# Turning the modulation rows with transposes and adding their four strips on VectorE

## The chip, the cores and the metric

The kernel runs on one core of a Trainium2 chip. The metric is the device time of one execution in microseconds; the number compared is the median of several runs.

## The reference

One layer of a hybrid backbone: a parallel mix of long convolution, latent attention and pooling, over 512 latent tokens and 256 context tokens, width 2048. The part that matters here is the modulation ahead of the first projection. For the conditioning vector `c` and for a learned one, `c_ctx`, three vectors come out of one weight matrix, and the normed tokens are scaled and shifted by them before `w_in`:

```python
def adaln(cond, w_ada, b_ada):
    mod = jax.nn.silu(cond) @ w_ada + b_ada
    shift, scale, gate = jnp.split(mod[:, None, :], 3, axis=-1)
    return shift, scale, gate
...
sh, sc, gt = adaln(c, w_ada[l], b_ada[l])
sh_c, sc_c, gt_c = adaln(c_ctx[None], w_ada[l], b_ada[l])
h_l = rmsnorm(x_l, norm_g[l]) * (1.0 + sc) + sh
h_c = rmsnorm(x_c, norm_g[l]) * (1.0 + sc_c) + sh_c
u_l = h_l @ w_in[l]
u_c = h_c @ w_in[l][:, OFF_KV:OFF_MLA_G]
```

## The kernel before

**Tiling.** Width 2048 is cut into 16 blocks (KT) of 128. The tokens lie transposed, a block j being 128 partitions by 512 tokens (`x_tile(j)`, in UG) and 256 context tokens (`c_tile(j)`). Every value that goes through TensorE in exact products is split into a high part and a low part of reduced type: ScalarE writes the high one, VectorE (or GpSimd) the low one by subtraction. Three products of such parts make one tile product.

**The stage concerned** is the first 130 us. A step j = 0 to 15 makes five tile products on TensorE (`tile(i, j)`, lines 1891 and 1897) for the columns of w_in that keys and queries need. The step takes `a_hi` and `a_lo` (tokens times scale, high and low), `hc_hi` and `hc_lo` (context), and `wa_hi` and `wa_lo` (weights). Norm and shifts are put in afterwards, so VectorE also keeps sums of squares (`rstd`, `rstd_c`) and sums of weights times shift (`shifted`, line 1211). From step 11 on ScalarE and VectorE also make the tokens for the next stage: `scale` (line 1240), `h_hi` on ScalarE (line 664), `h_lo` on VectorE (line 1247), two blocks a step.

**Modulation.** For a block b the weights (1 or 2 MB) come by DMA into one of three buffers `ada`. `ada_vectors(b)` on TensorE (line 1872) makes 16 products. Each has 32 columns of silu(c) as its stationary side, of which two are used (c and c_ctx), and goes to one of four strips of 32 partitions of bank ps[7]. So row 32s + r of the bank holds the part of strip s for vector r, and the four strips have to be added and the rows turned into a column per block. ScalarE copies the rows to SBUF (`rows_out`, `mod_rows`, line 670). Then `combine(b)` on TensorE (lines 1880 and 1881) does both at once: rows, stationary, times `comb`, a 128x2 matrix that selects and adds. ScalarE turns the result into scale and shift (`modulation`, lines 682 and 673), and then makes a_hi (line 637) and hc_hi. Blocks 0 and 1 (EARLY = 2) bring the scale alone, and their shifts come in one more block, number 12 (LATE), by `late_shifts`. Therefore `block_of(j)` is j up to 11 and j + 1 from 12 on.

**Order.** Every engine works through its own list in the order of the code, and waits on semaphores. On TensorE tile(0, j) is followed by `ada_vectors` of the next step's block and tile(1, j), then `combine` of it, then tiles 2 to 4. In step 10 the LATE block is done too. `at_work(n)` issues n idle products on ones, whose result nobody reads. At the start TensorE does four of them, `hidden(0)` (line 1917, the first layer of the filter network, which waits for `first_in` and for `feats`, shown as filter_steps), and ada_vectors(0), with two idle products in the middle.

On VectorE a step is: a_lo, hc_lo, the shifts, the sums, then h_lo of two blocks and `scale` of two. At the start it works on the sine arguments of the filter network (`hidden`, `reduced`, lines 1268 to 1277) ahead of the first a_lo. On GpSimd stands only wa_lo (line 577) in this stage. SP issues nearly all DMAs; ScalarE's queue issues the filter steps and the identity (lines 628 and 629). All loads of a step wait for the buffers of an earlier one.

The two lines of the combination before:

```python
if b >= EARLY:
    eng.matmul(ps[7][:, 0:2], rows[:, 0:P], comb[:], start=True, stop=True)
eng.matmul(ps[7][:, 2:4], rows[:, P:2 * P], comb[:], start=True, stop=True).then_inc(comb_mm, 1)
```

## Time and profile before

| | |
|---|---|
| median of 3 runs | 931.52 us (930.85 to 931.66) |
| profiled execution | 934.35 us, of which span 932.5 us |
| TensorE products busy | 916.4 us (98% of the span) |
| VectorE, ScalarE, GpSimd busy | 640.6, 395.8, 99.6 us |
| the 16 DMA engines, first 100 us | busy throughout, 367 to 423 GB/s |

The profile is of one execution; its times count from the start of the span. Each product of the float32 type shows as two instructions in the trace, a transpose as one. The ends of products are modelled, so the start of one to the start of the next says more than a duration.

### The profile page before, as it was taken

The page shows a single profiled execution, that of the slowest core. Times are in us where ns is not written, and L with a number is a line of the kernel's source. Part 1 is how long each engine was busy: PE and PEld are TensorE (multiplying, and loading weights), DVE is VectorE, ACT ScalarE, POOL GpSimd, SP SyncE. Part 2 cuts the span into 40 slices and gives each one's busy share as a digit, 9 for nine tenths or more (in the row PEclk, how much of TensorE's full clock was granted, in tenths as well). Part 3 has the DMA queues.
Part 4 walks back from the last instruction along what each step waited for, and adds up shares of the span by engine and source line. Part 5 has one row for each costly group of instructions (what it writes and reads, how often), then busy time and mean ns, then how long its engine had stood idle before and what let it go on. Part 6 is the DMA issues. An engine that isn't in the chain of part 4 may idle for free.

```text
span 932.5 us, 12223 instructions
## 1 busy us (share of the span) xinstructions
PE 916.4 (98%) x4878; PEld 760.6 (82%) x4878; DVE 640.6 (69%) x834; ACT 395.8 (42%) x614; POOL 99.6 (11%) x78
## 2 busy tenths in 40 slices
PE   9999999999999999999999999999999999999996
PEld 6777788888888888887788888889899888888885
DVE  5575997799987899855965854877777961424244
ACT  4654656535435443332234333554544541322124
POOL 2222200300003000000005720000000000202020
PEclk9999999999999999999999999999999999999998
DMA  9999923222322222476772251101010244233214
GB/s 367 414 419 423 401 104 102 91 79 95 110 79 91 69 85 74 148 292 225 269 287 90 91 175 52 57 23 57 1 57 1 91 171 191 91 102 119 96 46 181
DMA packets 29685, 137.88 MB, mean 148 GB/s; under 512 B 3483, under 2 KB 3995, under 8 KB 22716
## 3 DMA queue, kind: packets, MB, share of 16 engines
q1 hardware_dynamic: 29152, 136.44, 39.3%
q8 instruction: 39, 0.64, 0.3%
q10 hardware_dynamic: 476, 0.66, 0.2%
q14 instruction: 18, 0.15, 0.1%
HBM read 131.84 MB, written 4.19 MB: 146 GB/s over the span
## 4 chain that ended last, share of the span: by engine, by line
PE 87%; DVE 5%; DMA 3%; ACT 2%; issue 2%; POOLq 0%; SPq 0%; ACTq 0%
PE pp L1975 34%; PE pp L2289 19%; PE pp L2005 16%; PE pp L1891 6%; PE pp L1872 3%; DMA w_raw<-in_wb_dram 2%; PE pp L2252 2%; PE pp L1897 2%; DVE gate_acc L1329 1%; PE pp L2244 1%; PE pp L2243 1%; ACT U L962 1%; ACT w_hi L754 1%; DVE softmax_stats L1597 1%; DVE pt_lo L1612 0%
## 5 line engine op out<-in xcount | busy, mean ns | idle before, releaser
L1975 PE MATMUL pp<-h_hi,w_hi 128*128 128x512 f32 x544 | 213.9, 393 | 2.5 <-DVE w_lo L1317 2.4
L1975 PE MATMUL pp<-h_hi,w_lo 128*128 128x512 f32 x544 | 211.9, 389 | 0.0
L1975 PE MATMUL pp<-h_lo,w_hi 128*128 128x512 f32 x544 | 211.8, 389 | 0.0
L1317 DVE TENSOR_TENSOR w_lo<-w_raw,w_hi 128x1024 fp32r<-128x1024 f32 x68 | 88.0, 1295 | 77.9 <-ACT w_hi L754 77.4
L754 ACT ACTIVATE w_hi<-w_raw 128x1024 fp32r<-128x1024 f32 x68 | 71.8, 1056 | 141.6 <-PE pp L1975 90.1
L1975 PEld LDWEIGHTS pp<-h_hi,w_hi 128*128 128x128 f32 x544 | 102.2, 188 | 25.3 <-DVE w_lo L1317 4.4
L1975 PEld LDWEIGHTS pp<-h_hi,w_lo 128*128 128x128 f32 x544 | 102.1, 188 | 21.7
L1975 PEld LDWEIGHTS pp<-h_lo,w_hi 128*128 128x128 f32 x544 | 102.2, 188 | 20.5 <-issue 0.2
L2289 PE MATMUL pp<-wo_hi,m_hi 128*128 128x512 f32 x256 | 100.5, 393 | 0.0
L1632 DVE TENSOR_TENSOR wo_lo<-wo_raw,wo_hi 128x2048 fp32r<-128x2048 f32 x16 | 36.7, 2291 | 92.7 <-ACT wo_hi L993 92.7
L2289 PE MATMUL pp<-wo_hi,m_lo 128*128 128x512 f32 x256 | 99.6, 389 | 0.0
L2289 PE MATMUL pp<-wo_lo,m_hi 128*128 128x512 f32 x256 | 99.6, 389 | 0.0
L993 ACT ACTIVATE wo_hi<-wo_raw 128x2048 fp32r<-128x2048 f32 x16 | 30.6, 1915 | 89.4 <-PE pp L2289 89.4
L2289 PEld LDWEIGHTS pp<-wo_lo,m_hi 128*128 128x128 f32 x256 | 48.1, 188 | 10.3 <-issue 0.5
L2289 PEld LDWEIGHTS pp<-wo_hi,m_hi 128*128 128x128 f32 x256 | 48.1, 188 | 10.3 <-issue 0.5
L2289 PEld LDWEIGHTS pp<-wo_hi,m_lo 128*128 128x128 f32 x256 | 48.0, 188 | 10.1
L619 POOL TENSOR_TENSOR y<-y,gain 128x512 f32<-128x512 f32 x12 | 15.5, 1297 | 335.5 <-ACT out_tmp L1000 335.2
L1612 DVE TENSOR_TENSOR pt_lo<-pp,pt_hi 128x768 fp32r<-128x768 f32 x32 | 30.5, 953 | 24.9 <-ACT pt_hi L970 24.8
L970 ACT ACTIVATE pt_hi<-pp 128x768 fp32r<-128x768 f32 x32 | 26.0, 812 | 49.1 <-PE pp L2252 49.1
L962 ACT ACTIVATE U<-pp,softmax_stats 128x768 f32<-128x768 f32 x32 | 28.9, 903 | 27.5 <-DVE softmax_stats L1599 27.4
L1891 PE MATMUL pp<-a_hi,wa_hi 128*128 128x512 f32 x80 | 35.4, 443 | 0.0
L1329 DVE SCALAR_TENSOR_TENSOR gate_acc<-w_gate_raw,silu_c,gate_acc 128x2048 f32<-128x2048 f32 x15 | 35.2, 2346 | 0.0
(330 smaller groups left out, 1792.6 us busy)
## 6 DMA issues: line engine op xcount, KB each, us to landing
w_raw<-in_wb_dram SPq DMA_DIRECT2D x68, 512.0 KB, 3.3
ada_raw<-in_w_ada_dram SPq DMA_DIRECT2D x15, 2048.0 KB, 12.9
w_gate_raw<-in_w_gate_dram SPq DMA_DIRECT2D x16, 1024.0 KB, 5.1
wo_raw<-in_w_out_dram SPq DMA_DIRECT2D x16, 1024.0 KB, 4.7
wa_raw<-in_wa_dram SPq DMA_DIRECT2D x14, 320.0 KB, 7.3
y<-in_x_dram SPq DMA_DIRECT2D x4, 1024.0 KB, 7.9
UG<-in_xT_dram SPq DMA_DIRECT2D x7, 512.0 KB, 7.9
wh_raw<-in_w_heads_dram SPq DMA_DIRECT2D x4, 768.0 KB, 4.4
```

Of the source, the lines that this page charges most:

```text
L754: eng.activation(lane(wb_hi, n % 2), lane(wb_raw, n % KW), ACT.Copy).then_inc(wb_hi_done, 1)
L962: eng.activation(prob(n % 3).rearrange("p (a b) -> p a b", a=2), psum[:, 2 * (n % 2):2 * (n % 2) + 2, 0:384], ACT.Exp, bias=st[:, 4 * s + ...
L993: eng.activation(wo_high_[n % 2][:], wo_raw[n % 3][:], ACT.Copy).then_inc(wo_hi, 1)
L1317: eng.tensor_tensor(lane(wb_lo, n % KW), lane(wb_raw, n % KW), lane(wb_hi, n % 2), ALU.subtract).then_inc(wb_lo_done, 1)
L1329: eng.scalar_tensor_tensor(out=gate_acc[:], in0=w, scalar=c, in1=gate_acc[:], op0=ALU.mult, op1=ALU.add).then_inc(row_sums, 1)
L1612: eng.tensor_tensor(lo, psum[:, 4:6, :].rearrange("p a b -> p (a b)")[:, 0:LK].rearrange("p (k q) -> p k q", k=6), hi, ALU.subtract).then_ ...
L1632: eng.tensor_tensor(wo_low_[n % 3][:], wo_raw[n % 3][:], wo_high_[n % 2][:], ALU.subtract).then_inc(wo_lo, 1)
L1872: mm = eng.matmul(ps[7][32 * strip:32 * strip + 32, 256 - n:256], spread[:, 32 * kk:32 * kk + 32], ada[b % 3][:, kk * n:(kk + 1) * n], sta ...
L1891: mm = eng.matmul(ps[i][:], w, x, start=first and n == 0, stop=last and n == 2)
L1975: mm = eng.matmul(ps[i][:], w, x, start=(kk == 0 and m == 0), stop=(kk == KT - 1 and m == 2))
L2005: mm = eng.matmul(dst, w, x, start=first and m == 0, stop=last and m == 2)
L2289: mm = eng.matmul(psum[:, 4 * (b % 2) + tok, :], a, v[:, w:w + L], start=(kk == 0 and m == 0), stop=(kk == 15 and m == 2))
```

## The change

`combine(b)` now transposes the rows as they are, against the identity, into 128 or 256 columns of the same bank. A new function `strips(b)` on VectorE adds the four strips with one reduction into a small SBUF tile `strip_sums`, which ScalarE reads instead of PSUM. ScalarE's modulation waits for that sum. TensorE waits for the identity ahead of the first modulation products instead of in step 1; of its idle products one goes away in the middle of ada_vectors(0), and two are added behind it. The first half of the first scale weights is issued at the head of ScalarE's queue, no longer second on SP's.

```diff
@@ -98,7 +98,7 @@
         first_in, silu_c = alloc("first_in", 2 * KT + 131 + N_PAR + 2), alloc("silu_c", 2 * KT)
         cond, hf = first_in[:, 0:2 * KT], first_in[:, 2 * KT:2 * KT + 131]
         par, comb = first_in[:, 2 * KT + 131:2 * KT + 131 + N_PAR], first_in[:, 2 * KT + 131 + N_PAR:]
-        mod, scale_bias = alloc("mod", 4 * KT), alloc("scale_bias", KT)
+        mod, scale_bias, strip_sums = alloc("mod", 4 * KT), alloc("scale_bias", KT), alloc("strip_sums", 4)
         nrm, small, shift_cols = alloc("nrm", 8), alloc("hy_small", 8), alloc("shift_cols", 8)
         psum = ctx.enter_context(nc.psum_tensor("pp", [P, 8, 512], F32))
         ps = [psum[:, i, :] for i in range(8)]
@@ -312,7 +312,7 @@
 
         a_hi_done, a_lo_done = sem("a_hi_done"), sem("a_lo_done")
         root_done = sem("root_done")
-        ada_mm, rows_done, comb_mm = sem("ada_mm"), sem("rows_done"), sem("comb_mm")
+        ada_mm, rows_done, comb_mm, strips_done = sem("ada_mm"), sem("rows_done"), sem("comb_mm"), sem("strips_summed")
         mod_done, mod_scale, first_x_in, scaled = sem("mod_done"), sem("mod_scale"), sem("first_x_in"), sem("scaled")
         h_hi_done, h_lo_done = sem("h_hi_done"), sem("h_lo_done")
         wa_hi_done, wa_lo_done = sem("wa_hi_done"), sem("wa_lo_done")
@@ -416,7 +416,6 @@
                     eng.wait_ge(row_sums, shifts_of(j - 2))
                 eng.dma_start(wa_raw(j), t["wa"][j, :, :]).then_inc(wa_in[j % 2], 16)
 
-            eng.dma_start(ada[0][:, 0:1024], t["w_scale"][0, :, 0:1024]).then_inc(ada_in[0], 16)
             eng.dma_start(ada[0][:, 1024:2048], t["w_scale"][0, :, 1024:2048]).then_inc(hf_in, 16)
             load_wa(0)
             eng.dma_start(UG[:, 0:L], t["xT"][:, 0:L]).then_inc(first_x_in, 16)
@@ -625,6 +624,7 @@
 
         @block.scalar
         def _(eng):
+            eng.dma_start(ada[0][:, 0:1024], t["w_scale"][0, :, 0:1024]).then_inc(ada_in[0], 16)
             eng.dma_start(feats, t["feats"]).then_inc(feat_in, 16)
             eng.dma_start(mem["ident"][:], t["ident"]).then_inc(ident_in, 16)
 
@@ -670,22 +670,22 @@
                 eng.activation(rows[:, a:256], ps[7][:, a:256], ACT.Copy).then_inc(rows_done, 1)
 
             def shift_of(k, at_column):
-                eng.activation(mod[:, 4 * k:4 * k + 2], ps[7][:, at_column:at_column + 2], ACT.Identity,
+                eng.activation(mod[:, 4 * k:4 * k + 2], strip_sums[:, at_column:at_column + 2], ACT.Identity,
                                bias=par[:, P_BSH + k:P_BSH + k + 1], scale=1.0).then_inc(mod_done, 1)
 
             def modulation(j):
 
-                eng.wait_ge(comb_mm, block_of(j) + 1)
+                eng.wait_ge(strips_done, block_of(j) + 1)
                 if j in (10, 11):
 
                     eng.wait_ge(sum_mm, j - 9)
-                eng.activation(mod[:, 4 * j + 2:4 * j + 4], ps[7][:, 2:4], ACT.Identity, bias=scale_bias[:, j:j + 1],
+                eng.activation(mod[:, 4 * j + 2:4 * j + 4], strip_sums[:, 2:4], ACT.Identity, bias=scale_bias[:, j:j + 1],
                                scale=par[:, P_NG + j:P_NG + j + 1]).then_inc(mod_scale, 1)
                 if j >= EARLY:
                     shift_of(j, 0)
 
             def late_shifts():
-                eng.wait_ge(comb_mm, LATE + 1)
+                eng.wait_ge(strips_done, LATE + 1)
                 for k in range(EARLY):
                     shift_of(k, 2 * k)
 
@@ -1276,12 +1276,28 @@
                     link(eng.scalar_tensor_tensor(out=a, in0=r, scalar=-part, in1=a, op0=ALU.mult, op1=ALU.add))
                 eng.tensor_scalar(a, a, -PI_MAX, PI_MAX, ALU.max, ALU.min).then_inc(mlp_arg, 1)
 
+            def strips(b):
+                eng.wait_ge(comb_mm, b + 1)
+                if b:
+                    eng.wait_ge(mod_scale, b - (b > LATE))
+                if b > EARLY:
+                    eng.wait_ge(mod_done, b - EARLY + (EARLY - 1) * (b > LATE))
+                if b in (10, 11):
+                    eng.wait_ge(sum_mm, b - 9)
+                h = 1 if b < EARLY else 0
+                x = ps[7][:, h * P:2 * P].rearrange("p (h s r) -> p h r s", h=2 - h, s=4)[:, :, 0:2, :]
+                eng.tensor_reduce(strip_sums[:, 2 * h:4].rearrange("p (h r) -> p h r", r=2), x, AX.X, ALU.add).then_inc(strips_done, 1)
+
             hidden(0)
             reduced(0)
+            strips(0)
             first_tokens(0)
             first_context(0)
+            strips(1)
             hidden(1)
             for j in range(KT - 1):
+                if j:
+                    strips(block_of(j + 1))
                 first_tokens(j + 1)
                 first_context(j + 1)
                 if j == 0:
@@ -1309,6 +1325,7 @@
                     scale(2 * j - 20)
                     scale(2 * j - 19)
                 if j + 2 == LATE:
+                    strips(LATE)
                     for k in range(EARLY):
                         shifted(k)
 
@@ -1866,7 +1883,7 @@
                 n = P if b < EARLY else 256
                 for kk in range(KT):
                     if b == 0 and kk == 8:
-                        at_work(2)
+                        at_work(1)
                         eng.wait_ge(hf_in, 16)
                     strip = kk % 4
                     mm = eng.matmul(ps[7][32 * strip:32 * strip + 32, 256 - n:256], spread[:, 32 * kk:32 * kk + 32],
@@ -1877,8 +1894,8 @@
             def combine(b):
                 eng.wait_ge(rows_done, b + 1)
                 if b >= EARLY:
-                    eng.matmul(ps[7][:, 0:2], rows[:, 0:P], comb[:], start=True, stop=True)
-                eng.matmul(ps[7][:, 2:4], rows[:, P:2 * P], comb[:], start=True, stop=True).then_inc(comb_mm, 1)
+                    eng.transpose(ps[7][:, 0:P], rows[:, 0:P], mem["ident"][:])
+                eng.transpose(ps[7][:, P:2 * P], rows[:, P:2 * P], mem["ident"][:]).then_inc(comb_mm, 1)
 
             def tile(i, j):
                 first, last, s = j == 0, j == KT - 1, j % 2
@@ -1923,7 +1940,9 @@
             at_work(4)
             hidden(0)
             eng.wait_ge(silu_done, 2)
+            eng.wait_ge(ident_in, 16)
             ada_vectors(0)
+            at_work(2)
             combine(0)
             at_work(4)
             for j in range(KT):
@@ -1933,8 +1952,6 @@
                 else:
                     eng.wait_ge(wa_hi_done, 1)
                     eng.wait_ge(a_hi_done, 1)
-                if j == 1:
-                    eng.wait_ge(ident_in, 16)
                 for i in range(A_TILES):
                     if i == 2 and j:
                         eng.wait_ge(a_lo_done, 2 * j + 2)
```

On TensorE at the start, before; ada_raw_64 are the first scale weights, ones the idle products:

```order
L1872 MATMUL pp<-ada_raw_64,silu_spread 32x128 x8
L1857 MATMUL pp<-ones 128x128 x2
L1872 MATMUL pp<-ada_raw_64,silu_spread 32x128 x8
L1881 MATMUL pp<-first_in,mod_rows 128x2
L1857 MATMUL pp<-ones 128x128 x4
```

And the same place after:

```order
L1889 MATMUL pp<-ada_raw_64,silu_spread 32x128 x8
L1874 MATMUL pp<-ones 128x128
L1889 MATMUL pp<-ada_raw_64,silu_spread 32x128 x8
L1874 MATMUL pp<-ones 128x128 x2
L1898 MATMUL pp<-ident,mod_rows 128x128
L1874 MATMUL pp<-ones 128x128 x4
```

One idle product has moved behind the modulation products and one is added there, so two stand ahead of the combination, which has become a transpose.

On VectorE between steps 10 and 12, before; h_tmp<-UG is `scale`, the shifts on wa_first are the late ones:

```order
L1240 SCALAR_TENSOR_TENSOR h_tmp<-UG,mod,rstd 128x512 x2
L1211 SCALAR_TENSOR_TENSOR shift_x<-wa_first,mod,shift_x 128x640
L1211 SCALAR_TENSOR_TENSOR shift_c<-wa_first,mod,shift_c 128x384
L1211 SCALAR_TENSOR_TENSOR shift_x<-wa_first,mod,shift_x 128x640
L1211 SCALAR_TENSOR_TENSOR shift_c<-wa_first,mod,shift_c 128x384
L1191 SCALAR_TENSOR_TENSOR a_lo<-UG,mod,a_hi 128x512
```

And the same place after:

```order
L1240 SCALAR_TENSOR_TENSOR h_tmp<-UG,mod,rstd 128x512 x2
L1289 TENSOR_REDUCE strip_sums<-pp 128x4
L1211 SCALAR_TENSOR_TENSOR shift_x<-wa_first,mod,shift_x 128x640
L1211 SCALAR_TENSOR_TENSOR shift_c<-wa_first,mod,shift_c 128x384
L1211 SCALAR_TENSOR_TENSOR shift_x<-wa_first,mod,shift_x 128x640
L1211 SCALAR_TENSOR_TENSOR shift_c<-wa_first,mod,shift_c 128x384
L1289 TENSOR_REDUCE strip_sums<-pp 128x4
L1191 SCALAR_TENSOR_TENSOR a_lo<-UG,mod,a_hi 128x512
```

Two reductions stand there now: that of the LATE block between the scales and the late shifts, and that of block 13 directly ahead of step 12's a_lo.

On VectorE from step 12's h_lo to step 13's a_lo, after (before, the same rows without the reduction; steps 14 and 15 are alike):

```order
L1247 SCALAR_TENSOR_TENSOR h_lo<-h_tmp,mod,h_hi 128x512 x2
L1240 SCALAR_TENSOR_TENSOR h_tmp<-UG,mod,rstd 128x512 x2
L1289 TENSOR_REDUCE strip_sums<-pp 128x4
L1191 SCALAR_TENSOR_TENSOR a_lo<-UG,mod,a_hi 128x512
L1198 SCALAR_TENSOR_TENSOR hc_lo<-c_raw,mod,hc_hi 128x256
```

The reduction stands behind all of the work of the step before.

## Rows read from the trace of the kernel before

**Rows 1.** Two stretches: length; busy us (instructions) by engine; clock; DMA share; GB/s.
```profile
4.00:5.00 1.00, 1.00 (x2) 0.00 (x0) 0.00 (x0) 0.01 (x1) 0.00 (x0) 1.00 0.95 322
96.00:112.00 16.00, 16.00 (x146) 11.57 (x138) 15.87 (x21) 9.08 (x20) 5.29 (x3) 1.00 0.99 407
```

**Rows 2.** The chain that ended last: start us, us, what.
```profile
1.17 4.33 DMA ada_raw<-in_w_scale_dram
...
15.93 1.00 PE pp L1920 x2
...
58.94 0.12 PE pp L1880 x2
59.06 0.22 PE pp L1881 x2
59.28 0.80 PE pp L1891 x3
...
80.08 0.12 PE pp L1880 x2
...
101.50 0.69 PE pp L1891 x3
...
122.64 1.39 PE pp L1891 x6
```

**Rows 3.** VectorE in order of time: start us, us, instruction, idle time before.
```profile
95.66 0.88 DVE L1211 SCALAR_TENSOR_TENSOR shift_x<-wa_first,mod,shift_x 128x640 f32<-128x640 f32 x1
...
99.84 0.75 DVE L1191 SCALAR_TENSOR_TENSOR a_lo<-UG,mod,a_hi 128x512 fp32r<-128x512 f32 x1
...
102.56 2.70 DVE L1247 SCALAR_TENSOR_TENSOR h_lo<-h_tmp,mod,h_hi 128x512 fp32r<-128x512 f32 x2
...
106.56 0.75 DVE L1191 SCALAR_TENSOR_TENSOR a_lo<-UG,mod,a_hi 128x512 fp32r<-128x512 f32 x1
...
113.60 0.75 DVE L1191 SCALAR_TENSOR_TENSOR a_lo<-UG,mod,a_hi 128x512 fp32r<-128x512 f32 x1 [0.29 <-ACT a_hi L637]
...
120.81 0.74 DVE L1191 SCALAR_TENSOR_TENSOR a_lo<-UG,mod,a_hi 128x512 fp32r<-128x512 f32 x1
...
123.20 1.40 DVE L1247 SCALAR_TENSOR_TENSOR h_lo<-h_tmp,mod,h_hi 128x512 fp32r<-128x512 f32 x2
```

**Rows 4.** The chain of the attention stage: six transposes of 128x128.
```profile
608.92 0.65 PE pp L2252 x6
```

**Rows 5.** ScalarE in order of time around 79 us.
```profile
78.36 0.74 ACT L696 ACTIVATE wa_hi<-wa_raw 128x640 fp32r<-128x640 f32 x1 [2.00 <-DMA wa_raw<-in_wa_dram]
79.25 0.39 ACT L670 ACTIVATE mod_rows<-pp 128x256 f32<-128x256 f32 x1 [0.16 <-PE pp L1872]
```

**Rows 6.** All engines in order of time at the start.
```profile
0.73 0.62 ACTq L628 DMA_DIRECT2D filter_steps<-in_feats_dram  x1
...
3.45 1.96 PE L1917 MATMUL pp<-filter_steps,first_in 33*64 33x512 f32 x2 [0.33 <-DMA first_in<-in_first_dram]
5.45 0.80 DVE L1268 TENSOR_SCALAR filter_steps<-pp,first_in 64x512 f32<-64x512 f32 x1 [1.85 <-PE pp L1917]
...
6.64 1.22 PE L1857 MATMUL pp<-ones 128*128 128x128 f32 x4
...
9.35 0.42 DVE L1277 TENSOR_SCALAR filter_steps<-filter_steps 64x512 f32<-64x512 f32 x1
...
9.96 0.35 ACT L682 ACTIVATE mod<-pp,scale_bias,first_in 128x2 f32<-128x2 f32 x1
```

**Rows 7.** ScalarE in order of time: a modulation in the late steps.
```profile
112.38 0.35 ACT L682 ACTIVATE mod<-pp,scale_bias,first_in 128x2 f32<-128x2 f32 x1 [0.82 <-PE pp L1881]
```

**Rows 8.** Two groups on softmax_stats: duration ns min/median/max, first and last start, forms.
```profile
L1597 DVE TENSOR_REDUCE softmax_stats<-pp x32: 945/952/959, 577.2 to 742.9; 128x1 f32<-128x768 f32 x32
L1599 DVE TENSOR_SCALAR softmax_stats<-softmax_stats x32: 153/154/156, 578.2 to 743.9; 128x1 f32<-128x1 f32 x32
```

**Rows 9.** GpSimd in order of time beside VectorE's h_lo.
```profile
102.42 1.63 POOL L577 TENSOR_TENSOR wa_lo<-wa_raw,wa_hi 128x640 fp32r<-128x640 f32 x1 [4.45 <-ACT wa_hi L696]
```

## The prediction

> **What bounds the kernel now.** I read three views: busy time by stretch, the chain that ended last, and each engine's instructions in order of time. The change touches only the first 130 us, the stage in which sixteen steps j build the modulation vectors and the first projections; what follows is fed by TensorE without a gap, so a delay at the end of the stage goes into the total undiminished.
>
> Two engines are full in the last part of it. From 96 to 112 us TensorE is busy for 16.00 of 16 us and VectorE for 15.87 [rows 1]. The chain of waits goes through TensorE: the tile products of step 12 start at 101.50 and those of step 15 at 122.64, so one step takes 7.05 [rows 2]. VectorE is nearly as tight: it starts a_lo of steps 12, 13, 14 and 15 at 99.84, 106.56, 113.60 and 120.81, and only the third of them names an idle time, 0.29 [rows 3]. TensorE needs that a_lo (ready 0.7 after its start) at 101.50, 108.55 and so on: the slack is 1.0 to 1.3 us. So two questions decide: what TensorE saves, and what VectorE's order now costs.
>
> **Combination on TensorE.** Before, two float32 products with two columns each take 0.12 + 0.22 us, and the tile products behind them take 0.80 where three others take 0.69: 0.45 in all [rows 2]. After, two transposes stand there. The kernel has the same form elsewhere, six in 0.65 us, 0.11 each [rows 4]. That is 0.22, and up to 0.33 if the products behind them are late as before. The gain is 0.12 to 0.23 per combination; I take 0.18, 2.7 us for the 15 combinations with both halves.
>
> **How much of this arrives by 88 us.** The weights wa_raw come by DMA. In the step near 78 us ScalarE waited 2.00 us for them and began at 78.36, and the row copy behind it began at 79.25, 0.16 after ScalarE fell free [rows 5]. TensorE needs that copy for its next combination at 80.08 [rows 2], and the copy takes 0.39: 0.44 us later than now it would be late. If TensorE runs ahead of the DMA, which is busy throughout, it can be at most 0.16 + 0.44, about 0.55 us, ahead there; then it waits for the row copy. Two more combinations up to 88 us bring 0.36, so I take 0.9 as the lead at the combination of block 11. Bounds: 1.5 if the DMA also comes earlier, or a delay of 0.5 if the start loses much (next part).
>
> **The start.** The first half of the scale weights moves from SP's queue to the head of ScalarE's, ahead of the filter steps and the identity. It needed 4.33 us from its issue at 1.17 to landing [rows 2]. It may now be issued at 0.73, where ScalarE's queue starts [rows 6], worth up to 0.44. But hidden(0) waits for the filter steps, which now lie behind 512 KB. It ran from 3.45 [rows 6]; with the pace of 322 GB/s at 4 to 5 us [rows 1], 512 KB more ahead of the steps take 1.6, so they come at about 5.0. Bounds: 3.45 if they overtake, 5.7 if SP's queue takes turns. The Trainium skill (DMA: Bandwidth & Descriptors, Queues, rings and completion order) says that each DMA engine goes round-robin between the queue rows that have work, packet by packet. By that rule the transfer would share the engines with SP's second half and take nearly twice as long, and the filter steps would come at the late bound. No row here shows such sharing of large transfers.
>
> From there two paths run. hidden(0) takes 1.96, and VectorE's sine arguments on 64 rows run from 5.45 to 9.77 [rows 6]; the new strips(0) stands behind them, so the modulation begins at about 5.0 + 1.97 + 4.35 + 0.25 = 11.6, against 9.96. On TensorE ada_vectors(0) follows hidden(0) and the new wait for the identity: start 1.5 later, one idle product less in its middle (-0.6, half of the 1.22 of two [rows 6]), two more before the combination (+0.6, as they take 1.2 and the row copy hid 0.4 of it anyway), one product fewer. That meets the other path at about 11.2. So the first tile products start about 1.6 later than now. Of this some comes back, since TensorE runs at half pace at first: hidden(0) takes 1.96 at 3.45, and hidden(1), of as many columns, 1.00 at 15.93 [rows 2, 6]. TensorE has fewer gaps after the filter steps now, and I count 0.7 back. At j = 1 VectorE comes to strips(2) only after its sums, 0.3 more. Net +1.2 at 27 us. Nine combinations then bring 1.6, and TensorE is 0.4 to 0.55 ahead at 79 us: the cap of the part before is just reached, so this loss is mostly hidden by waiting that the DMA would have forced anyway.
>
> The Trainium skill (TensorE: Matmul & The Clock Gate, Part 4) adds that transposes do not count as activity for the clock. By that rule the start would stay slow longer; see the rivals.
>
> **VectorE's new place in the chain.** strips(b) is queued behind everything that VectorE does for the step before. In steps up to 11 that costs little: VectorE is idle when the combination comes, and the 0.2 to 0.25 falls into a slack of 1 us. From step 10's end on it isn't idle. Before, ScalarE made mod and a_hi while VectorE still worked, and a_lo followed at once. Now VectorE finishes the two scale() instructions, then sums the strips, then must wait for ScalarE's modulation and a_hi before a_lo. Behind it are queued the shifts, sums and h_lo of the step, so nothing fills the gap.
>
> The price of one such gap: the modulation began at 112.38 and a_lo at 113.60, 1.22 [rows 3, 7]. The sum of strips: no row shows a reduction of 16 elements. Lower bound 0.15 (128x1, SBUF), upper 0.95 (768 elements from PSUM) [rows 8]; I take 0.20, near the small one, and 0.05 for the hand-over. ScalarE now reads SBUF instead of PSUM, which I credit with 0.05. Gap: 1.4 (1.2 to 1.6 with half of the doubt on either side).
>
> Now the steps, relative to the lead of 0.9. VectorE's path in step 11 gains 0.25 before the scales. strips(LATE) and the first late shift that waits for it put shifted(0), now at 95.66 [rows 3], 0.5 later: ScalarE's late shifts, the first of them about as long as a modulation (0.35 [rows 7]), now stand behind VectorE's scales, and TensorE's ada_vectors(13) waits for them too, but no longer than VectorE's path below. So shifted(0) is 0.75 late. Then a_lo of step 12: 99.84 + 0.75 + 1.4 = 102.0, late by 2.15. Step 13: 6.72 of work between starts, plus 1.4, 110.1 (late by 3.55). Step 14: 6.75 of work (7.04 less the 0.29), 118.3 (4.7). Step 15: 7.21 of work, 126.9 (6.1). The work does not shrink: the pair of h_lo instructions takes 2.70 while GpSimd's wa_lo runs beside it from 102.42, and 1.40 at 123.20 without it [rows 3, 9]; GpSimd still starts after ScalarE's h_hi, so the two still meet.
>
> TensorE can start step 15 at 126.9 + 0.70 = 127.6 instead of 122.64, +4.95. Less the lead of 0.9: +4.05. What TensorE would save in steps 11 to 15 vanishes, since it waits for VectorE. VectorE is 1.1 nearer to TensorE after that, and I add 0.1 for the change to the next stage. **Sum: +4.2 us.** The profiled execution was 934.35 (span 932.5 and 1.85 around it), so it would be 938.5; the median of the runs lay 2.8 lower at 931.52, so the forecast is 935.7. A measurement of this kernel can tell about 0.2% (1.9 us) from no change: 929.7 to 933.4 counts as the same.
>
> **Rivals.** First, the start costs more: the filter steps at 5.7 and nothing back from the pace give +2.6 and a delay instead of a lead at 88 us, about 1.4 to 2.4 worse: 937.5. For it: everything at the start hangs on one small transfer. Against: the DMA cap hides a part.
>
> Second, on the other side: the gap on VectorE is covered. If a_lo needs no more than its slack of 1.0 to 1.3 in steps 12 to 15, for instance because GpSimd's subtraction now falls into VectorE's waiting and gives 1.3 back per step, the gap of 1.4 is paid by that and only TensorE's savings remain: 0.9, about 0.3 more in each of steps 12 to 15 less the waits, some 1 us faster: 930.5. It decides at a gap of 0.35, the spare of 7.05 against 6.72. For it: contention of 1.3 is there. Against: the order of ScalarE and GpSimd moves with VectorE's.
>
> Third, the cover is partial (half of the steps): +1.5, 933.0.
>
> Fourth, TensorE stays at its lower pace up to the combination of step 3, since transposes keep it up less than products do: half pace from 15 to 21 us costs 6, of which the cap hides little: 939.5 and more.
>
> Fifth, the transposes save nothing (0.45 again). It changes the lead to 0, and so the time to 936.6; it lies inside my range.
>
> **Chances.** Forecast (with the fifth) 0.72; first 0.10; second 0.07; third 0.07; fourth 0.04. The forecast's own range is a gap of 1.2 to 1.6 over five places (1.0 each way) and a lead of 1.5 to -0.5: 934.1 to 938.1. With the first case and the upper part of the third it is 933.0 to 938.3, which leaves out the second, the fourth and half of the third. Slower by over 0.2%: 0.84; the same: 0.09; faster: 0.07.
>
> **What would show it.** Right: in the profile after, VectorE idles before each a_lo of steps 12 to 15, about 1.2 us released by ScalarE's a_hi, directly behind the reduction, and TensorE waits for a_lo in steps 12 to 15, some 1.3 us apiece; transposes at 0.11 spacing; a wait for the filter steps at the start. Wrong: TensorE's steps stay 7.05 or less apart up to 123 us, or h_lo pairs shrink to 1.40.

## The result, and the profile of the changed kernel

The changed kernel takes 940.69 us (median of four: 937.12, 942.23, 942.03, 939.35), the kernel before 931.59 beside it. The ratio on record, formed from all executions and not from the two medians, is 1.009 (95% interval 1.0071 to 1.011): slower, with the predicted sign, but by 9.1 us where 4.2 were forecast, and outside the range of 933.0 to 938.3. Five executions of the later runs that lasted over 1,000 us (two of the kernel before, two of e12, one of e10) are left out of every number here.

The profiled execution took 937.12, the shortest of the four; that of before took 934.35, which is 2.8 above its median. So the two profiles differ by only 2.8 us while the medians differ by 9.1. Two questions follow: what happens in the first 140 us, and what makes a profile and a median differ. I begin with the stage.

The longest waits of TensorE in the profile after (line waiting, what it waited for, us in total, times, longest):

```profile
PE pp L1908 <- DVE a_lo L1191: 4.3, 4, 1.6
PE pp L1934 <- DMA filter_steps<-in_feats_dram: 3.1, 1, 3.1
...
PE pp L1889 <- ACT mod L673: 1.6, 1, 1.6
```

The first row is for the most part the predicted one. Of its four waits for VectorE's a_lo, three are those of steps 13, 14 and 15 (1.08, 1.07 and 1.62); the fourth, 0.52, is that of step 2. In step 12 TensorE does not wait for a_lo, where the prediction had a wait of some 1.3: its loss lies a little earlier, in the third row, the wait for the late shifts in step 11 (1.59), which the prediction named and gave no time of its own.

VectorE's instructions of step 12 and the beginning of 13, in order of time (start, us, line, operation; in brackets the idle time before, and what ended it). Beside the rows of before [rows 3]:

```profile
105.06 2.70 DVE L1247 SCALAR_TENSOR_TENSOR h_lo<-h_tmp,mod,h_hi 128x512 fp32r<-128x512 f32 x2
107.68 1.40 DVE L1240 SCALAR_TENSOR_TENSOR h_tmp<-UG,mod,rstd 128x512 f32<-128x512 f32 x2
109.00 0.16 DVE L1289 TENSOR_REDUCE strip_sums<-pp 128x4 f32<-128x16 f32 x1
110.46 0.75 DVE L1191 SCALAR_TENSOR_TENSOR a_lo<-UG,mod,a_hi 128x512 fp32r<-128x512 f32 x1 [1.29 <-ACT a_hi L637]
```

The reduction takes 0.16, and then VectorE stands idle for 1.29. From the start of the reduction to the start of a_lo it is 1.46, where before a_lo followed the scales with no gap. The same idle time, 1.29, stands before a_lo in each of the steps 12 to 15. The chain of waits walks through exactly this gap (start, us, what):

```profile
109.08 0.09 DVE strip_sums L1289
...
109.20 0.39 ACT mod L682
109.59 0.07 ACT mod L673
...
109.70 0.73 ACT a_hi L637
...
110.46 0.46 DVE a_lo L1191
```

VectorE hands a sum of 16 numbers per partition to ScalarE, ScalarE makes scale, shift and a_hi, and VectorE, which could have worked on something else, waits at a_lo. The four a_lo of steps 12 to 15 start at 102.33, 110.46, 118.59 and 127.26 (before 99.84, 106.56, 113.60, 120.81), so the step has grown from 7.0 to 8.1 and once 8.7. Step 15 and the end of the stage, from the chain of waits after:

```profile
128.16 1.62 PE pp L1908 x6
129.79 1.95 PE pp L1927 x16
...
135.43 4.79 PE pp L1992 x21
```

Step 15 begins at 128.16 instead of 122.64 [rows 2], 5.5 later, and the next stage at 135.43 instead of 129.39, 6.0 later.

The combination has become cheaper, as TensorE's rows for block 7 show:

```profile
57.33 1.93 PE L1889 MATMUL pp<-ada_raw,silu_spread 128*32 128x256 f32 x32
...
59.99 0.27 PE L1897 MATMUL pp<-ident,mod_rows 128*128 128x128 f32 x1
60.10 0.27 PE L1898 MATMUL pp<-ident,mod_rows 128*128 128x128 f32 x1
60.13 0.48 PE L1908 MATMUL pp<-a_hi,wa_hi 128*128 128x512 f32 x1
...
64.14 1.93 PE L1889 MATMUL pp<-ada_raw,silu_spread 128*32 128x256 f32 x32
71.14 1.93 PE L1889 MATMUL pp<-ada_raw,silu_spread 128*32 128x256 f32 x32
78.16 1.93 PE L1889 MATMUL pp<-ada_raw,silu_spread 128*32 128x256 f32 x32
```

The transposes start 0.11 apart, and the modulation products of two neighbouring steps 6.82 apart (57.33 to 64.14) where it was 7.05: 0.22 a step. But the next two steps are 7.00 and 7.02 again, and the granted clock is at its upper level (2.4 GHz) in all of this stretch. Something else sets the pace from 64 us to 78 us; the experiments e6 and e10 find it.

The start, as TensorE and ScalarE lived it (rows of before: [rows 6]):

```profile
4.76 0.23 ACT L699 ACTIVATE silu_c<-first_in 128x32 f32<-128x32 f32 x1 [1.25 <-DMA first_in<-in_first_dram]
6.17 1.94 PE L1934 MATMUL pp<-filter_steps,first_in 33*64 33x512 f32 x2 [3.05 <-DMA filter_steps<-in_feats_dram]
8.42 1.08 PE L1889 MATMUL pp<-ada_raw,silu_spread 128*32 128x128 f32 x16 [0.32 <-issue]
...
13.97 0.47 PE L1908 MATMUL pp<-a_hi,wa_hi 128*128 128x512 f32 x1 [0.77 <-ACT a_hi L637]
...
15.09 1.08 PE L1889 MATMUL pp<-ada_raw,silu_spread 128*32 128x128 f32 x32
...
28.85 0.47 PE L1908 MATMUL pp<-a_hi,wa_hi 128*128 128x512 f32 x1 [0.52 <-DVE a_lo L1191]
```

hidden(0) waits 3.05 for the filter steps and starts at 6.17 instead of 3.45. The first tile products come at 13.97, before at 11.43: 2.5 later. The modulation products of block 1 take 1.08 at 15.09. Before, the same products at 12.99 took 1.94, half that pace, so 0.9 comes back here, and 0.4 with the three tile products ahead of them (1.12 from 13.97 to 15.09, before 1.56 from 11.43 to 12.99). The start of block 2's products is then 1.25 late (22.14 against 20.89). Then two steps lose time again: at 28.85 TensorE waits for the a_lo of step 2, since VectorE's sum of block 2's strips (at 26.49, a_lo at 27.95) stood behind the long work on sines and squares. At the products of block 3 the changed kernel is 1.8 late (29.72 against 27.94).

### The profile page after: what moved, and what is told of

Same layout as the page of the kernel before. It is cut to its first block, busy times and chain, and to the rows that moved or that the text cites. A ratio compares the mean times of both kernels' runs of the same rounds, so it can differ in the third digit from the quotient of the medians.

```text
span 935.3 us, 12197 instructions
## 1 busy us (share of the span) xinstructions
PE 912.0 (98%) x4848; PEld 755.7 (81%) x4848; DVE 642.1 (69%) x851; ACT 396.0 (42%) x614; POOL 101.8 (11%) x78
## 4 chain that ended last, share of the span: by engine, by line
PE 80%; DVE 6%; ACT 2%; issue 2%; POOLq 0%; DVEq 0%; ACTq 0%
PE pp L1992 38%; PE pp L2306 19%; PE pp L2022 16%; PE pp L2269 2%; DVE h_lo L1247 1%; PE pp L2261 1%; PE pp L2260 1%; ACT U L962 1%; DVE softmax_stats L1614 1%; DVE pt_lo L1629 0%; PE pp L2091 0%; PE pp L1908 0%; PE pp L2039 0%; PE pp L2038 0%; PE pp L2144 0%
## 6 DMA issues: line engine op xcount, KB each, us to landing
ada_raw<-in_w_ada_dram SPq DMA_DIRECT2D x15, 2048.0 KB, 12.6
```

## Experiments

All times are medians, with the number of executions, and the ratio against executions of the kernel before on the same chip (formed from all executions, so it is not quite the quotient of the medians). "Stage" is how much later than before (140.38) ScalarE starts one fixed instruction behind the stage, the w_hi of line 754 that stands directly ahead of the single w_hi of line 824 (w_hi is the high part of the next projection's weights). It is read from one profile of each. How far one profile can be trusted is seen in e5 and e12, whose code is that of before up to step 15: their last modulation products start at 116.42 and 116.37 where those of before start at 116.22. So 0.2 in this column is nothing, and the three profiles of the changed kernel differ by 2.2. The two kernels that appear again (e1 and e11, e12) are repeats.

| kernel | median, executions | ratio (95%) | stage |
|---|---|---|---|
| changed | 940.69 (4) | 1.009 (1.0071 to 1.011) | +6.05 |
| e1, changed again | 939.05 (6) | 1.0082 (1.0054 to 1.011) | +6.39 |
| e11, changed, third | 940.04 (6) | 1.0086 (1.0055 to 1.0117) | +8.25 |
| e3, combination alone | 939.05 (6) | 1.0069 (1.0041 to 1.0096) | +5.57 |
| e4, sum before the scales | 933.17 (12) | 1.0017 (0.9999 to 1.0035) | +0.72 |
| e2, start alone | 932.92 (12) | 1.0015 (0.9999 to 1.0032) | +1.21 |
| e7, first load alone | 933.18 (10) | 1.0013 (1.0004 to 1.0022) | +2.31 |
| e6, combination, sum early | 931.3 (11) | 1.0 (0.9984 to 1.0016) | +0.08 |
| e8, e4 and load behind the filter steps | 934.39 (11) | 1.0031 (1.0015 to 1.0046) | +2.16 |
| e5, delay only | 937.09 (5) | 1.0058 (1.0046 to 1.007) | +6.02 |
| e12, delay again | 938.28 (8) | 1.006 (1.004 to 1.0079) | +5.96 |
| e9, before with half loads | 930.61 (10) | 0.9985 (0.9967 to 1.0003) | -0.27 |
| e10, e6 with half loads | 931.17 (9) | 0.9982 (0.9963 to 1.0001) | -0.52 |

### e1: the changed kernel again

No edit. It is the same code in the company of the next three.

> The changed kernel once more, unaltered. Its first four runs spread over 5 us (937.1 to 942.2), while those of the kernel before spread over 1. Theory D (VectorE's order alone is the cause): a constant cost of 5.5 us at the last step's tile products, so runs near 937 to 939 and a spread of about 1. Theory S (a part of the cost is made anew in every run at the start, by the pace of TensorE or of the first transfers): the spread of some 5 us comes back, the median near 940.5, and in a profile of a slow run the first step or two start later than 13.97 and 22.14 us.

Measured: 938.39, 938.55, 945.02, 939.55, 938.0, 939.65. The stage loses 6.39, a_lo of steps 12 to 15 at 102.67, 110.82, 118.95 and 127.61. The stage's loss repeats in this profile, which is of the execution of 938.39. Where the spread of seven microseconds comes from it doesn't show. A spread of about 1 (Theory D) is refuted, but the median is not at 940.5 either (Theory S); e11 takes that up.

### e2 and e3: the start alone, the combination alone

e2 has the start of the changed kernel and the combination of before:

```diff
-            eng.dma_start(ada[0][:, 0:1024], t["w_scale"][0, :, 0:1024]).then_inc(ada_in[0], 16)
...
         def _(eng):
+            eng.dma_start(ada[0][:, 0:1024], t["w_scale"][0, :, 0:1024]).then_inc(ada_in[0], 16)
             eng.dma_start(feats, t["feats"]).then_inc(feat_in, 16)
...
-                        at_work(2)
+                        at_work(1)
...
+            eng.wait_ge(ident_in, 16)
             ada_vectors(0)
+            at_work(2)
```

> The kernel before with the start of the changed one alone: first scale weights at the head of ScalarE's queue, wait for the identity ahead of ada_vectors(0), one idle product in its middle and two behind it; the combination is still the product with comb. Theory D: the start costs at most 1 us in the median and adds no spread, 931.5 to 932.5. Theory S: +2.5 us or more (the first tile products start near 14.0 instead of 11.43), and the spread of some 4 us is here, so 934 to 936.

e3 is the changed kernel with these lines put back (the load leaves ScalarE's queue again), the wait for the identity directly ahead of combine(0):

```diff
+            eng.dma_start(ada[0][:, 0:1024], t["w_scale"][0, :, 0:1024]).then_inc(ada_in[0], 16)
...
-                        at_work(1)
+                        at_work(2)
...
-            eng.wait_ge(ident_in, 16)
             ada_vectors(0)
-            at_work(2)
+            eng.wait_ge(ident_in, 16)
             combine(0)
```

> The transposes and VectorE's sum alone: first scale weights on SP's queue and two idle products in the middle as before, none ahead of the combination; the wait for the identity stands directly ahead of the first combination, which needs it now. Theory D: nearly all of the loss stays, VectorE idles 1.29 us before a_lo in steps 12 to 15, about +4.2 us, 935.7. Theory S: +3 us at most (the gaps less the savings on TensorE), with a spread below 1.5.

e2 takes 932.92 (1.0015), its stage loses 1.21. This lies between the two theories: 1.4 in the median, more than 1 and less than 2.5, and its executions spread from 932.08 to 937.18. Its steps in the last part are 7.05 as before (a_lo at 100.96, 107.75, 114.80, 122.02), hidden(0) waits 2.9 for the filter steps, and block 1's products have the full pace early:

```profile
14.98 1.08 PE L1872 MATMUL pp<-ada_raw,silu_spread 128*32 128x128 f32 x32
```

e3 takes 939.05 (1.0069), its stage loses 5.57, more than either theory had (4.2 and at most 3). TensorE's waits in it:

```profile
PE pp L1908 <- DVE a_lo L1191: 4.2, 4, 1.6
PE pp L1889 <- DMA ada_raw<-in_w_ada_dram: 1.1, 1, 1.1
```

So nearly the whole loss belongs to the combination. The second row is new: without the loss at the start, TensorE comes to block 9's weights 1.1 before they have landed. The first profile of the whole change names no such wait, since there TensorE comes late from the start. The two parts don't add up (5.57 + 1.21 = 6.8 against 6.05 to 6.4), because the loss at the start is partly waiting that the DMA forces anyway: the changed kernel is 1.95 behind e3 at the products of block 3 (29.72 against 27.77) and 0.77 behind at those of block 9 (71.14 against 70.37).

### e4: the sums ahead of the scales

This keeps everything of the change but VectorE's order from the end of step 10 on. The sum of the next step's strips moves from behind the two `scale` instructions to ahead of them, that of the LATE block too, and that of block 13 to between the two late shifts:

```diff
-                if j:
+                if 0 < j < 11:
                     strips(block_of(j + 1))
...
+                if j + 2 == LATE:
+                    strips(LATE)
+                if 10 < j < KT - 2:
+                    strips(block_of(j + 2))
                 if j >= 10:
                     scale(2 * j - 20)
                     scale(2 * j - 19)
                 if j + 2 == LATE:
-                    strips(LATE)
-                    for k in range(EARLY):
-                        shifted(k)
+                    shifted(0)
+                    strips(block_of(j + 2))
+                    shifted(1)
```

> The changed kernel, but from block 12 on VectorE sums the strips ahead of the two scales (and for block 13 between the two late shifts) instead of behind them, so that ScalarE makes scale and a_hi while VectorE still works; nothing else is moved. Theory D: the idle time before a_lo of steps 12 to 15 falls from 1.29 to under 0.4 and the time by about 5 us. Theory S: the same idle time goes, but some 3 us and the spread remain, so near 935.5.

It takes 933.17 (1.0017), and the stage loses 0.72 instead of 6.05. VectorE's rows at the place that was shown above:

```profile
106.30 0.16 DVE L1289 TENSOR_REDUCE strip_sums<-pp 128x4 f32<-128x16 f32 x1
106.38 1.40 DVE L1240 SCALAR_TENSOR_TENSOR h_tmp<-UG,mod,rstd 128x512 f32<-128x512 f32 x2
107.76 0.75 DVE L1191 SCALAR_TENSOR_TENSOR a_lo<-UG,mod,a_hi 128x512 fp32r<-128x512 f32 x1
```

```profile
PE pp L1912 <- DVE a_lo L1191: 0.5, 1, 0.5
```

The same reduction, with the same 0.16, but now 1.40 of scales lie between it and a_lo, ScalarE's 1.2 us run beside them, and a_lo has no idle time before it. Of TensorE's four waits for a_lo only that of step 2 is left, 0.5, so those of steps 13 to 15 (3.8 together) are gone, and the wait for the late shifts has shrunk from 1.59 to 0.34. These two make 5.0 of the 5.3 us of stage that the order is worth. The instructions are the same, only in another order. As the order was changed in all these places at once, what each is worth alone is not shown.

### e5: is a delay at the end of the stage passed on undiminished?

The kernel before with 26 idle products ahead of step 15's tiles:

```diff
+                if j == KT - 1:
+                    for _ in range(26):
+                        eng.matmul(ps[7][:, 0:P], ones[:], ones[:], start=True, stop=True)
```

> The kernel before with 26 idle products on TensorE ahead of step 15's first tile products, which nobody reads: a bare delay of some 5.5 us at the place where the changed kernel had collected it, with nothing else changed. Theory P (a delay at the end of the stage is passed on undiminished, and the stage with the gate weights at 404 to 490 us adds its own, random part that has nothing to do with the change): the fastest run is 5.5 above the fastest of before (930.8), 936.3, and the median lies 1 to 2 above that. Theory M (the later stages absorb or multiply a delay): the fastest run is under 935 or over 938.

It takes 937.09 (1.0058; 936.88 to 937.62), 5.3 more than before on the same chip (931.82) with a delay of 6.0 in the stage. The median lies only 0.2 above the shortest, not 1 to 2 as Theory P had it. The shortest ones differ by 6.0 (936.88 and 930.85). So a delay of this size is passed on nearly one to one, and a pure delay of the changed kernel's size gives 937, not 940.7. At this point it seemed that the change cost 2 to 3 us beyond its delay. e12 weakens that.

### e6, e8: what the transposes are worth

e6 is the kernel before with transposes, strip sums in e4's order, and the start as it was, but for the wait for the identity, which stands ahead of the first combination. Its main edit against before:

```diff
-                    eng.matmul(ps[7][:, 0:2], rows[:, 0:P], comb[:], start=True, stop=True)
-                eng.matmul(ps[7][:, 2:4], rows[:, P:2 * P], comb[:], start=True, stop=True).then_inc(comb_mm, 1)
+                    eng.transpose(ps[7][:, 0:P], rows[:, 0:P], mem["ident"][:])
+                eng.transpose(ps[7][:, P:2 * P], rows[:, P:2 * P], mem["ident"][:]).then_inc(comb_mm, 1)
```

> The transposes with VectorE's sum ahead of the scales, and the start as in the kernel before. If the start is the last loss of the version with the early sum (+0.7 at the end of the stage with the changed start), this one should end the stage 0.3 to 1.0 us ahead of the kernel before: 930.0 to 931.3. If the DMA of the modulation weights caps the lead (they land as late as before), it is at the kernel before within 0.4.

It takes 931.3 (1.0, 0.9984 to 1.0016): no gain, though steps of 6.82 in place of 7.05 save 0.22 each. TensorE at block 9's weights:

```profile
70.84 1.93 PE L1893 MATMUL pp<-ada_raw,silu_spread 128*32 128x256 f32 x32 [1.35 <-DMA ada_raw<-in_w_ada_dram]
```

Without the wait these products would have started at 69.5, 0.7 ahead of before (70.21). Their weights were issued 0.26 earlier than before (56.63 against 56.89), but took 14.1 instead of 12.9:

```profile
ada_raw<-in_w_ada_dram SPq DMA_DIRECT2D x1, 2048.0 KB, 14.1
```

They landed at 70.73, and a lead of 0.7 became a delay of 0.6. The later steps win that back, and the stage ends 0.08 later than before. The saving is real, and the wait for the DMA takes it back.

e8 is e4 (the changed start with its wait for the identity ahead of ada_vectors(0)) with the filter steps put at the head of ScalarE's queue, then the scale weights, then the identity:

```diff
+            eng.dma_start(feats, t["feats"]).then_inc(feat_in, 16)
             eng.dma_start(ada[0][:, 0:1024], t["w_scale"][0, :, 0:1024]).then_inc(ada_in[0], 16)
-            eng.dma_start(feats, t["feats"]).then_inc(feat_in, 16)
             eng.dma_start(mem["ident"][:], t["ident"]).then_inc(ident_in, 16)
```

> The changed kernel with the early sum, and on ScalarE's queue the filter steps first, then the scale weights, then the identity. Theory Q: hidden(0) starts at 3.6 to 4.2, the modulation products wait for the identity, which now is last (about 6), and the first steps are some 1.5 us earlier than in the version with the filter steps second. Time: 930.0 to 931.5, unless the DMA caps the lead.

934.39 (1.0031), where 930.0 to 931.5 had been expected. The identity was expected at about 6 and came at 8.4, so the wait has only changed its name:

```profile
3.37 1.96 PE L1938 MATMUL pp<-filter_steps,first_in 33*64 33x512 f32 x2 [0.26 <-DMA first_in<-in_first_dram]
...
8.43 1.08 PE L1893 MATMUL pp<-ada_raw,silu_spread 128*32 128x128 f32 x16 [3.10 <-DMA ident<-in_ident_dram]
```

hidden(0) is back at 3.37, and the identity, now the small load behind the large one, keeps ada_vectors(0) until 8.43, the same time as in the changed kernel (8.42). In the changed kernel the identity lands at 8.34 too, just behind the end of hidden(0), so two small loads are late there and bringing one forward gains nothing.

### e7: the load alone, without the idle products

```diff
-            eng.dma_start(ada[0][:, 0:1024], t["w_scale"][0, :, 0:1024]).then_inc(ada_in[0], 16)
...
         def _(eng):
+            eng.dma_start(ada[0][:, 0:1024], t["w_scale"][0, :, 0:1024]).then_inc(ada_in[0], 16)
             eng.dma_start(feats, t["feats"]).then_inc(feat_in, 16)
```

> The kernel before with one edit: the first half of the first scale weights at the head of ScalarE's queue, ahead of the filter steps and the identity. Theory Q (the two queues take turns, and the filter steps lie behind 512 KB): hidden(0) starts at about 6.1 instead of 3.45 and the stage ends about 1.2 late, 932.7: the whole of the start's cost. If instead the idle products and the identity make it, under 0.4 late.

```profile
4.98 0.23 ACT L699 ACTIVATE silu_c<-first_in 128x32 f32<-128x32 f32 x1 [1.48 <-DMA first_in<-in_first_dram]
5.90 1.94 PE L1917 MATMUL pp<-filter_steps,first_in 33*64 33x512 f32 x2 [2.79 <-DMA filter_steps<-in_feats_dram]
...
15.12 1.94 PE L1872 MATMUL pp<-ada_raw,silu_spread 128*32 128x128 f32 x32
```

933.18 (1.0013), stage +2.31 in the profile, where 1.2 had been expected. The queue move alone delays the filter steps as in the changed kernel, and it is most of the cost of the start: ada_vectors(0) begins at 7.77, 2.1 later than before (5.63), in the changed kernel 2.8 later. There hidden(0) itself is 0.3 later than in e7, and 0.3 more lies between its end and ada_vectors(0), which waits for the identity that lands at 8.34. The other half of that part, the identity's wait and the idle products, seems the good one: with it (e2) block 1's products take 1.08, without it 1.94 (at 15.12). But this pace changes from one execution to the next. In e5 and e12, whose start is that of the kernel before (1.94), the same products take 1.08 and 1.36:

```profile
13.59 1.08 PE L1872 MATMUL pp<-ada_raw,silu_spread 128*32 128x128 f32 x32 [0.26 <-DMA ada_raw<-in_w_scale_dram]
```

```profile
13.24 1.36 PE L1872 MATMUL pp<-ada_raw,silu_spread 128*32 128x128 f32 x32
```

All six profiles with the changed idle products and wait have 1.08; of the eight without them one has. So this half makes the full pace the rule there. Of the 0.9 that came back in the changed kernel, the comparison with e5 would leave nothing. In the profiles of e2 and e7 the difference is 1.1 us of stage; in the medians of twelve and ten executions it isn't seen (932.92 against 933.18).

### e9 and e10: is it the modulation weights that hold the pace?

Both load only half of each block's 2 MB, and the products of the second half read the first half again, so blocks from 2 on come out with other values; all instructions stay. e9 is the kernel before with this, e10 is e6 with it.

```diff
-                dst, src = (ada[b % 3][:, 0:2048], t["w_scale"][b]) if b < EARLY else (ada[b % 3][:], t["w_ada"][b - EARLY])
+                dst, src = (ada[b % 3][:, 0:2048], t["w_scale"][b]) if b < EARLY else (ada[b % 3][:, 0:2048], t["w_ada"][b - EARLY][:, 0:2048])
...
-                                    ada[b % 3][:, kk * n:(kk + 1) * n], start=kk < 4, stop=kk >= KT - 4,
+                                    ada[b % 3][:, kk * n % 2048:kk * n % 2048 + n], start=kk < 4, stop=kk >= KT - 4,
```

> The kernel before, but of each 2 MB block of modulation weights only the first half is loaded, and the products of its second half use the first again (the modulation is wrong in value, all instructions stay). Theory C (the modulation weights' arrival is the only thing that keeps TensorE from running ahead between 60 and 80 us, and in the kernel before it is just hidden): steps stay 7.05 apart and the stage ends within 0.5 of before. If other loads or engines set the pace, nothing changes either, and the next run tells.

> The version with transposes and the early sum and the old start, with the same halved loads. Theory C: steps stay 6.82 apart throughout, no wait for ada_raw, and the stage ends 1.2 to 1.6 us earlier than with whole loads, so 9 steps' savings of 0.22 show that whole loads swallow. If something else caps the lead (the copy of the rows behind the late weights wa_raw, as the prediction had it), the time stays as it was, near 931.3.

e9 takes 930.61 (0.9985), its stage ends 0.27 earlier than that of before, and it is 0.3 ahead already at block 2's products (20.60 against 20.89); its steps stay 7.05. So TensorE hardly waits for these loads there. In e10 the wait of 1.35 is gone, and the steps stay 6.82 up to 77 us:

```profile
63.18 1.93 PE L1893 MATMUL pp<-ada_raw,silu_spread 128*32 128x256 f32 x32
70.00 1.93 PE L1893 MATMUL pp<-ada_raw,silu_spread 128*32 128x256 f32 x32
76.82 1.93 PE L1893 MATMUL pp<-ada_raw,silu_spread 128*32 128x256 f32 x32
```

(62.58 and 70.84 in e6, 8.26 apart with the wait.) So the DMA is what swallows the transposes' saving, and e6 names the load. The edit itself frees all loads (the DMA share from 60 to 80 us falls from 1.02 to 0.74), so e10 alone could not say which. The gain at the end of the stage is smaller than I had put it, 0.6 against e6, and in the medians it isn't seen (931.17 against 931.3). Two losses of e10 can be placed. By the products of block 3 it is 0.86 behind e6 (28.76 against 27.90), and 0.7 of that is the pace of block 1's products, 1.94 in e10 and 1.25 in e6, which varies from execution to execution (e7). And in the step from 76.82 it loses 0.4: VectorE's sums of squares take 2.65 instead of 1.49, as GpSimd's wa_lo now runs beside them (from 77.11, before from 79.17), and TensorE starts the product behind its transposes only when they are done (79.99).

### e11 and e12: is there a cost beyond the delay?

e11 is the changed kernel once more, e12 is e5's kernel once more, on the same chip.

> The changed kernel again, for its spread. So far ten runs, 937.1 to 945.0, half of them over 939.3, though the stage that was changed ends 6.0 to 6.4 late in both profiles. Theory R (the surplus over 937 is chance in the gate-weight stage and the same for every kernel): a median near 938 and an excess over the fastest like that of the kernel before (about 0.8 in the median). Theory V (the changed kernel meets that stage worse): again a median 2 us or more above 937.

> The bare delay again on the same chip as the changed kernel, for the same question. Its five runs were 936.9 to 937.6. Theory R: a few of the new runs lie above 939 and the median at 937.0 to 938.5. Theory V: they stay within 1 us of 937, and the changed kernel's do not.

e11: 941.91, 947.63, 939.43, 940.47, 939.62, 938.73. e12: 936.81, 937.24, 937.31, 937.6, 938.96, 939.54, 940.94, 942.71. The two answers don't agree: e12 (median 938.3, three above 939) is as Theory R had it, and e11's median of 940.0, 3.0 above 937, is as Theory V had it. The pure delay also spreads up to 942.7, where e5's five ended at 937.6, so a spread of this kind is not the changed kernel's own; whether it is larger there stays open. Two sources can be seen in the profiles. The first is in the stage. In e11's profile TensorE waits for the modulation weights in spite of its late start, and the DMA moved less than before in the same stretches (TensorE, its loads, VectorE, ScalarE, GpSimd, clock, DMA share, GB/s):

```profile
73.08 1.93 PE L1889 MATMUL pp<-ada_raw,silu_spread 128*32 128x256 f32 x32 [0.80 <-DMA ada_raw<-in_w_ada_dram]
```

```profile
20.00:40.00 20.00, 19.35 (x166) 13.38 (x166) 13.59 (x26) 11.30 (x25) 5.37 (x3) 1.00 1.00 402
40.00:60.00 20.00, 19.63 (x173) 14.35 (x171) 13.97 (x24) 11.91 (x26) 4.04 (x3) 1.00 1.01 393
```

The same stretches of before:

```profile
20.00:40.00 20.00, 20.00 (x176) 14.54 (x175) 12.15 (x21) 11.91 (x27) 4.84 (x3) 1.00 1.01 417
40.00:60.00 20.00, 20.00 (x176) 14.56 (x175) 15.41 (x21) 11.07 (x26) 5.02 (x3) 1.00 1.02 421
```

From 40 to 60 us it is 393 against 421 GB/s, and in the first profile of the changed kernel it was 412. The stage loses 8.25 instead of 6.05: 0.6 of the 2.2 stands there already at block 3's products (30.29 against 29.72), and 1.3 comes with the waits for the weights up to block 9 (73.08 against 71.14).

The second is much later, between 404 and 490 us, where the gate weights (w_gate) are loaded and VectorE multiplies them (15 instructions of 2.35 each) between the splits of the projection weights, w_lo. Outside this stretch the profiles of all runs stay parallel within 0.5 us from the stage's end on. Take the profiled time less the stage's shift: 931.0 to 931.2 in changed, e2, e4, e6, e7 and e10, 931.6 in e5, 932.0 in e1, but 934.35 in before, 933.7 in e11, 933.9 in e3, 935.8 in e8 and e9, and 936.8 in e12. In every profile of the second group TensorE waits for w_lo there (before 2.4, e11 1.8, e3 1.4, e8 and e9 2.7, e12 3.6), and in e1 0.5. These waits are a half to three quarters of the surplus; the rest shows under no name. In before and in e12:

```profile
PE pp L1975 <- DVE w_lo L1317: 2.4, 3, 1.1
```

```profile
PE pp L1978 <- DVE w_lo L1317: 3.6, 4, 1.3
```

In changed, e2, e4 to e7 and e10 there is no such row. Identical kernels (e5 and e12, changed and e11) fall on either side, so no edit makes it. It costs 2.6 to 5.7 us in an execution; what decides it is open.

## Why the prediction was right on VectorE's gap and wrong on the lead and the median

**VectorE's gap: right.** The price was put at 1.4 (sum 0.20, chain 1.22) and measured 1.46 (sum 0.16, idle 1.29). For the sum the Trainium skill (VectorE: DVE Perf Modes, The TRN2 errata) has a rule, 120 cycles and one per element from PSUM at 0.96 GHz, which would have made it 0.14 by estimate; the row with 0.16 is near it, and it changes nothing in the outcome. The 0.05 credited to ScalarE for reading SBUF rests on no row, and the runs show none: the modulation takes 0.39 from strip_sums where it took 0.35 from PSUM [rows 7]. The late times of a_lo, forecast against TensorE's place at block 11, were 2.15, 3.55, 4.7 and 6.1. They came out as 2.5, 3.9, 5.0 and 6.45 by the clock, and as 2.0, 3.4, 4.5 and 5.9 against that place, where the kernel was 0.5 late. h_lo stayed at 2.70, as said, and from the combination of block 11 to step 15 the changed kernel lost 5.0 where 4.95 was forecast. e4 shows that this order is 5.3 of the 6.05 us of stage. The second and the third rival, a gap that is covered wholly or half, are refuted by the idle 1.29 before each a_lo. One sign of being right failed: TensorE waits for a_lo in steps 13 to 15 and not in step 12.

**The combination: right in its size (0.22, taken 0.18), wrong in what arrives.** The fifth rival, no saving, falls too. But this is the first step that failed: "I take 0.9 as the lead at the combination of block 11". The kernel was 0.5 behind there (the products after it start at 88.29 instead of 87.76), 1.4 worse, and just at the prediction's own lower bound. Of the 1.4, the start is 0.6, a second late sum on VectorE 0.3 and the cap 0.4. Three errors lie in it:

1. *The place of the cap.* I looked for it at the row copy and at wa_raw near 79 us [rows 5], and found 0.55 of room. The nearer one was the modulation weights themselves, one step earlier. Their DMA and their first use in the kernel before:

```profile
56.89 0.43 SPq L410 DMA_DIRECT2D ada_raw<-in_w_ada_dram  x1
...
70.21 1.93 PE L1872 MATMUL pp<-ada_raw,silu_spread 128*32 128x256 f32 x32
```

```profile
ada_raw<-in_w_ada_dram SPq DMA_DIRECT2D x1, 2048.0 KB, 12.9
```

56.9 + 12.9 = 69.8, and the products start at 70.21: room for 0.4 only. Even that is one execution's: in e5 and e12, the same code up to there, the same load takes 13.6, and TensorE waits 0.39 and 0.38 for it. And the landing doesn't come earlier when TensorE is faster, since the DMA is busy throughout (share 1.02 from 60 to 80 us): in e6 it is issued 0.26 earlier and lands 0.9 later. After, the load is issued at 58.45, takes 12.6 and lands at 71.05; the products start at 71.14. That of block 10 is issued at 65.29, takes 12.7 and lands at 77.99, and its products start at 78.16. (The steps of 7.00 and 7.02 are this limit; they cost 0.4 together. The idle of under 0.2 in each doesn't show as a wait, since the ends of products are modelled.)

2. *The size of the start.* Forecast +1.2 at 27 us, measured +1.8 at step 3. The filter steps came at 6.17, behind even the late bound of 5.7, and so the first tile products at +2.5 for +1.6. The pace gave 1.3 back for 0.7, against a profile of before that was itself at the slow end (e7). VectorE's sums in front of strips(2) and strips(3) cost 0.76 and 0.33 (steps of 7.58 and 7.15 in place of 6.82), where 0.3 was taken for one. This is the first rival in its larger part: the start did cost more, and there was a delay at 88 us instead of a lead. It priced the stage's loss at 6.0 (937.5), which is what the stage then lost, but by luck, for the amounts are others: the steps came later, the pace gave something back, and a part of the rest lay behind step 15. Of the two bounds for the filter steps, that with shared engines was the right one, and I took the middle. first_in shows the sharing: it is issued first on SP's queue at 0.72 in both kernels, but a load of 512 KB is now issued on the other queue at 0.73, where before nothing large followed until 1.17, and it lands 1.3 (e7: 1.6) later. The Trainium skill (DMA: Bandwidth & Descriptors, Queues, rings and completion order) states that each DMA engine goes round-robin between the queue rows that have work; the late first_in agrees with that.

3. *A count.* "Nine combinations then bring 1.6": between 30 and 79 us lie seven, and 7 x 0.22 is 1.5, which with 1.8 to make up leaves no lead at all.

**The end of the stage: mis-sized.** I added 0.1 behind step 15; it is 0.5. By the chain, the first six products of step 15 take 1.62 for 1.39, and the products behind them (L1927), which sum the shifts over the partitions, 1.95 for 1.68. Half of it can be placed. By order of time step 15 of the kernel before starts at 122.48, not 122.64, so 0.16 is a difference between the two views. And the shift sums on VectorE now end at 129.73, when TensorE has finished the six products (about 129.61) and must wait for them (129.79); before, they ended at 123.27 and TensorE came at 123.87. The remaining 0.2 is not placed. In sum the stage loses 6.0 for 4.2: 1.4 from the lead, 0.05 from the gap, 0.4 here.

**From the profile to the median: the second step that failed.** The stage alone would have stayed inside the range (931.52 + 6.05 is 937.6). "The median of the runs lay 2.8 lower" was carried over unchanged, as a property of profiling. It was waiting in the profiled execution, which can be seen in it (w_lo, 2.4). The changed kernel's profile has none. And the sum had no term for the spread of the executions: the changed kernel's first median lies 3.6 above its shortest execution, that of before 0.7. Of the 4.9 us by which the forecast missed 9.1, 2.1 lie between the shortest executions (6.3 instead of 4.2) and 2.8 in this spread. The honest form is: shortest execution plus shift, plus a spread of up to several us that both have. For the kernel before, 80 executions run from 930.76, with a median of 931.66; for the changed one, 16 from 937.12, with a median of 939.6. The shortest ones differ by 6.4, what the stage gives. The medians differ by 7.9. What is between, 1.5 us, I can only partly place: the changed kernel's stage itself varies (6.05, 6.39, 8.25), and the delayed kernel, which has none of this, has a median of 937.3 in 13 executions, 5.6 over before. e3, which has the late sums but not the changed start, has the same excess as the changed kernel: its median lies 2.6 above its shortest execution (936.42), that of e4 1.4, that of e6 0.8. Whether the changed kernel meets the late stretch in a worse state than the others stays open.

**The fourth rival, a lower pace through transposes, is refuted:** the granted clock is 1.00 in the steps (2.4 GHz), they last 6.82, and at the start, where the clock column doesn't tell the pace (see below), block 1's products take 1.08, not 1.94, in every profile of the changed kernel. The Trainium skill (TensorE: Matmul & The Clock Gate, Part 4) says that transposes do not count as activity for the clock; two of them, 0.11 us apart, in each step of 6.82 gave no sign of a cost here.
